# Two extra 2 MB expert slots, and a shorter routing chain, ahead of the mixture of experts

## The chip, the cores and the metric

The kernel runs on one core of one Trainium2 chip, as one launch. The metric is the device time of one execution in microseconds, the lower the better. Engines are called by the names of the profile: PE (TensorE), PEld (its weight loads), DVE (VectorE), ACT (ScalarE), POOL (GpSimd) and SP (SyncE, which here only issues DMAs).

## What is computed

Two transformer blocks over 256 tokens of width 1024, in float32. The change lies at the seam to the last stage, the mixture of experts of the second block, which is this, cut to its core (4 groups of 8 experts, 2 chosen per token, each expert 1024 to 512 to 1024):

```python
p_group = softmax(h @ w_router_group)              # 256 x 4
g_idx, g_gate = argmax(p_group), max(p_group)
logits_sel = (h @ w_router_expert) of group g_idx  # 256 x 8
top_vals, top_idx = top_k(logits_sel, 2)
comb = one_hot(g_idx) * softmax(top_vals) * g_gate
for g in range(G):
    hg = einsum('td,edf->tef', h, w_gate[g])
    hu = einsum('td,edf->tef', h, w_up[g])
    act = silu(hg) * hu * comb[:, g, :, None]
    y = y + einsum('tef,efd->td', act, w_down[g])
```

Here h is the RMS norm of the residual x, and y is added to x.

## The kernel before

Up to 1139 us of the span the kernel runs four dense feed-forward layers and three mixers. Their weights pass through a ring of raw pieces; ACT rounds each piece to fp32r (`high`), DVE takes the rest (`low`), and PE multiplies three times (`product`, L242 to L246). The last of them, `mix_out`, adds its result to x. Then comes the expert stage.

**The experts.** Each of the 32 experts has 6 MB of weights, which are loaded as three pairs of 2 MB: two pairs hold half the rows of gate and up, one pair holds down. A pair is two DMAs of 1 MB, issued by SP in `pair_load` (L1951). The 32 experts are always all loaded, in the order of a plan. The pairs go through `pair_ring`, six slots of 2 MB, laid over `low`, `high`, `raw` and a part of `scratch`. In `moe_sp` SP issues the first pair once the mixer's second tile of h is there (`h_ready`, L1676), the next two once the last piece is split, the next three once PE has used the last piece. Then it waits for the plan (`last_batch`, L1932), and issues each later pair when PE has used the pair six before it (`pair_used`).

**A batch** is four experts ("items") of 32 token slots each. PE gathers a batch's tokens with a product by a one-hot table `picks` (`turn_batch`, L1996, results in `BATCH_X`), ACT copies that to `batch_x` (L2078), and for each item PE computes gate and up (`gate_up`, L2017), ACT and DVE the SiLU and the product, PE the turn (L2024) and `down` (L2036). At the end of a batch `scatter` (L2047) spreads the results, and DVE adds them to x (L2130). All batches are iterations of one `Fori` loop on each engine; here there are eight. Inside a batch, the gather for the next one comes after the second item's gate and up.

**The routing chain** stands between x and the first `picks`. PE turns x (`x_turn_pe`, L389), ACT writes the rounded transpose `hT_high` (L399), DVE `hT_low` (L409), and PE multiplies by the router in 48 matmuls of 36 columns (`route_pe`). DVE then scales the logits (L1776), finds the group and the two experts with their one-hot `takes` (L1818), and signals `picked` (L1822). PE counts and ranks the tokens by expert with five products (L1925, `ranks`; the trace has two records for each); DVE meanwhile writes h, the normed x (`normed_x`, L377, two of 128x1024), and the shares (L1826 to L1831). With the ranks, DVE works out the item and place of every choice (L1834 to L1857), including overflow items for experts with more than 32 tokens, and writes `picks` and `shares` (`picks_of`, L1886 to L1905). After that it makes the plan (L1870 to L1883). The tables lie in `proj`, which is free by then. Most steps wait for the one before, through the helper `step`.

## Time and profile before

| | us |
|---|---|
| median of 3 runs | 1667.09 (1665.92 to 1668.19) |
| profiled execution, device time | 1667.57 |
| its span | 1665.8 |
| PE busy in the span | 1466.4 (88%) |
| DVE busy | 751.3 (45%) |
| ACT busy | 615.1 (37%) |

The page cuts the span into 40 slices of 41.6 us, and gives for each the busy share of every engine, the granted PE clock, the busy share of the 16 DMA engines and the GB/s that they moved. The dense part fills the first 28 slices, the experts the last 12. A busy PE is not PE at its peak, since a matmul's recorded time overlaps its neighbours'. Times in the timelines are counted from the span's start.

### The profile page before, as it was taken

To read this page: it belongs to the slowest core of one execution; us is meant where nothing else is said; L and a number is where in the kernel's file an instruction comes from. 1 tells how busy PE (TensorE), PEld (TensorE's weight loads), DVE (VectorE), ACT (ScalarE), POOL (GpSimd) and SP (SyncE) were. 2 spreads that over 40 slices of the span, in tenths; PEclk is the share of its full clock that TensorE was granted. 3 is DMA by queue.
4 is the path that set the end of the run, shared out by engine and by line. 5 is a ranking of instruction groups with operands and counts; after the bars stand their busy time and mean duration, and the time that the engine had idled before them with its cause. 6 is when DMAs were issued, how large, how long until landed. Compare 5 with 4: busy or idle time off the path is not lost.

```text
span 1665.8 us, 22441 instructions
## 1 busy us (share of the span) xinstructions
PE 1466.4 (88%) x8732; PEld 1124.5 (68%) x8732; DVE 751.3 (45%) x985; ACT 615.1 (37%) x783; POOL 32.6 (2%) x69
## 2 busy tenths in 40 slices
PE   7999999599999999999999999998676767766766
PEld 5888887588888888877788888777544424434433
DVE  4445647845455554565455454685520221221111
ACT  5343545344344543465654344664010011011010
POOL 4000000000000000000010000000000000000000
PEclk9999989999999999999999999999798888979788
DMA  6646544035645555544355555554599999999997
GB/s 214 218 158 214 190 156 171 27 102 186 218 153 200 177 192 186 190 164 151 127 161 199 200 171 182 176 179 189 199 417 417 418 419 417 418 417 418 418 417 298
DMA packets 170764, 396.54 MB, mean 238 GB/s; under 512 B 9507, under 2 KB 107891, under 8 KB 154336
## 3 DMA queue, kind: packets, MB, share of 16 engines
q1 hardware_dynamic: 169152, 392.20, 63.3%
q0 software_dynamic: 1440, 3.72, 0.9%
q8 instruction: 28, 0.46, 0.1%
q14 instruction: 16, 0.13, 0.0%
q10 hardware_dynamic: 128, 0.03, 0.0%
HBM read 393.83 MB, written 1.05 MB: 237 GB/s over the span
## 4 chain that ended last, share of the span: by engine, by line
PE 69%; DMA 11%; SPq 9%; DVE 6%; ACT 3%; issue 2%; DVEq 0%; ACTq 0%
PE psum L244 19%; PE psum L246 19%; PE psum L245 19%; DMA pair_ring<-in_w_exp_up 9%; SPq L1951 9%; PE psum L1996 4%; PE psum L2017 2%; PE psum L2036 1%; DMA pair_ring<-in_w_exp_down 1%; PE psum L526 1%; DVE low L239 1%; DVE hT_low L409 1%; ACT hT_high L399 1%; ACT high L235 1%; PE psum L1162 1%
## 5 line engine op out<-in xcount | busy, mean ns | idle before, releaser
L239 DVE TENSOR_TENSOR low<-raw,high 128x2048 fp32r<-128x2048 f32 x179 | 406.4, 2289 | 138.3 <-ACT high L235 135.3
L244 PE MATMUL psum<-high,hT_high 128*128 128x512 f32 x1088 | 437.2, 402 | 13.8 <-DVE low L2264 5.0
L246 PE MATMUL psum<-high,hT_low 128*128 128x512 f32 x1088 | 428.0, 393 | 0.0
L245 PE MATMUL psum<-low,hT_high 128*128 128x512 f32 x1088 | 427.2, 393 | 0.0
L235 ACT ACTIVATE high<-raw 128x2048 fp32r<-128x2048 f32 x179 | 338.3, 1911 | 61.3 <-PE psum L246 56.7
L244 PEld LDWEIGHTS psum<-high,hT_high 128*128 128x128 f32 x1088 | 206.7, 190 | 59.6 <-issue 8.9
L246 PEld LDWEIGHTS psum<-high,hT_low 128*128 128x128 f32 x1088 | 206.4, 190 | 44.9
L245 PEld LDWEIGHTS psum<-low,hT_high 128*128 128x128 f32 x1088 | 207.1, 190 | 40.8
L2017 PE MATMUL psum<-pair_ring,scratch 128*32 128x256 f32 x2048 | 141.8, 428 | 57.5 <-DMA pair_ring<-in_w_exp_up 56.2
L2017 PEld LDWEIGHTS psum<-pair_ring,scratch 128*32 128x32 f32 x2048 | 67.6, 120 | 129.7 <-DMA pair_ring<-in_w_exp_up 77.8
L636 ACT ACTIVATE aT_high<-psum 128x512 fp32r<-128x512 f32 x40 | 23.9, 598 | 323.0 <-PE psum L526 323.0
L674 DVE TENSOR_TENSOR aT_low<-psum,aT_high 128x512 fp32r<-128x512 f32 x40 | 27.7, 692 | 255.3 <-ACT aT_high L636 255.3
L244 PE MATMUL psum<-high,aT_high 128*128 128x512 f32 x352 | 137.4, 390 | 0.2
L246 PE MATMUL psum<-high,aT_low 128*128 128x512 f32 x352 | 137.0, 389 | 0.0
L245 PE MATMUL psum<-low,aT_high 128*128 128x512 f32 x352 | 137.0, 389 | 0.0
L2036 PE MATMUL psum<-pair_ring,scratch 128*32 128x256 f32 x1024 | 82.8, 478 | 44.9 <-DMA pair_ring<-in_w_exp_down 40.7
L2087 ACT ACTIVATE scratch<-psum 32x256 f32<-32x256 f32 x64 | 23.8, 373 | 200.3 <-PE psum L2036 199.9
L2109 DVE TENSOR_TENSOR scratch<-scratch,psum 128x128 f32<-128x128 f32 x32 | 9.2, 287 | 186.8 <-ACT scratch L2082 186.8
L2036 PEld LDWEIGHTS psum<-pair_ring,scratch 128*32 128x32 f32 x1024 | 40.8, 131 | 72.8 <-issue 52.6
L2082 ACT ACTIVATE scratch<-psum 128x128 f32<-128x128 f32 x32 | 8.9, 277 | 212.1 <-PE psum L2017 212.1
L1996 PE MATMUL psum<-proj,h 128*128 128x128 f32 x288 | 71.1, 408 | 8.2 <-DVE proj L1904 8.2
L1996 PEld LDWEIGHTS psum<-proj,h 128*128 128x128 f32 x288 | 69.4, 335 | 12.9 <-issue 12.9
(317 smaller groups left out, 1173.7 us busy)
## 6 DMA issues: line engine op xcount, KB each, us to landing
pair_ring<-in_w_exp_gate SPq DMA_DIRECT2D x64, 1024.0 KB, 22.1
pair_ring<-in_w_exp_up SPq DMA_DIRECT2D x64, 1024.0 KB, 22.8
pair_ring<-in_w_exp_down SPq DMA_DIRECT2D x64, 1024.0 KB, 22.4
raw<-in_ffn_w_gate SPq DMA_DIRECT2D x88, 512.0 KB, 4.1
raw<-in_ffn_w_up SPq DMA_DIRECT2D x88, 512.0 KB, 5.3
raw<-in_ffn_w_down SPq DMA_DIRECT2D x88, 512.0 KB, 4.0
raw<-in_gla_w_in SPq DMA_DIRECT2D x24, 512.0 KB, 4.6
raw<-in_sb_w_in SPq DMA_DIRECT2D x24, 512.0 KB, 4.6
```

Source lines behind the costliest of these rows:

```text
L235: act.activation(high[:, p % RING, :], raw_of(p), ACT.Copy).then_inc(rounded, 1)
L239: dve.tensor_tensor(low[:, p % RING, :], raw_of(p), high[:, p % RING, :].bitcast(F32), ALU.subtract).then_inc(split, 1)
L244: pe.matmul(psum_out, lhs_high, rhs_high, start=start, stop=False, skip_group_check=True)
L245: pe.matmul(psum_out, lhs_high, rhs_low, start=False, stop=False, skip_group_check=True)
L246: return pe.matmul(psum_out, lhs_low, rhs_high, start=False, stop=stop, skip_group_check=True)
L636: act.activation(flat(aT_high), TURN_A, ACT.Copy).then_inc(a_high, 1)
L674: dve.tensor_tensor(flat(aT_low), TURN_A, flat(aT_high).bitcast(F32), ALU.subtract).then_inc(a_low, 1)
L1951: sp.dma_start(dst, src).then_inc(pair_landed[i % PAIRS], 16)
L1996: ins = pe.matmul(BATCH_X[:, k * P:(k + 1) * P], h[:, tt, :].rearrange("p (n k) -> p k n", k=KD)[:, k, :], picks[:, tt * P:(tt + 1) * P], ...
L2017: ins = pe.matmul(out_rows, batch_x[:, kk, j * SLOTS:(j + 1) * SLOTS], w[:, :, k, c * P:(c + 1) * P], start=kk == 0, stop=kk == KD - 1, sk ...
L2036: ins = pe.matmul(ITEM_Y[q * SLOTS:(q + 1) * SLOTS, :], item_aT[:, c * SLOTS:(c + 1) * SLOTS], w[:, c, q * QUARTER:(q + 1) * QUARTER], sta ...
L2087: ins = act.activation(batch_y[j * SLOTS:(j + 1) * SLOTS, q * QUARTER:(q + 1) * QUARTER], ITEM_Y[q * SLOTS:(q + 1) * SLOTS, :], ACT.Copy)
```

## The change

- **Memory.** `gate`, `act_tok` and `proj` now stand right behind `aT_high` and `aT_low`, and `extra_pairs`, two slots of 2 MB, is laid over these five. `hT_high` and `hT_low` become one buffer, and the routing tables move from `proj` to `route_tables`, laid over it; `iota` and `group_pad` move to `levels`.
- **Loads.** SP issues pairs 6 and 7 first, into the extra slots, at the point where pair 0 was issued; then pair 0, and pairs 1 to 5 behind the waits that they had. Pairs 8 to 11 wait for the first four uses and not for the plan; their experts, 2 and 3, are fixed. From the second batch on, the ring of six serves alone, and each pair waits for the use of the pair six before.
- **Router product.** For each k one matmul of 72 columns (high and low router side by side) and one of 36, instead of three of 36: 32 matmuls for 48. DVE adds the two halves before it scales.
- **Order.** ACT takes the second tile's mean square after its transpose. DVE writes h ahead of the wait for the logits, not behind `picked`.
- **First batch.** Its slots are 32 times the expert plus the rank; a rank of 32 or more is pushed out of range by `too_far`. `picks_of(0)` thus comes right after the ranks, and the item arithmetic runs behind it.
- **PE program.** The first batch is written out, and the loop runs over the others; PE reads the plan after the first batch.


The diff, cut to its core:

```diff
+EXTRA = 2
...
-        hT_high = sb("hT_high", [P, KD, TOKENS], F32R)
-        hT_low = sb("hT_low", [P, KD, TOKENS], F32R)
+        hT = sb("hT", [P, 2, KD * TOKENS], F32R)
+        hT_high, hT_low = (hT[:, i, :].rearrange("p (k n) -> p k n", k=KD) for i in range(2))
+        route_tables = nc.alloc_sbuf_tensor_at("route_tables", [P, 2 * KD * TOKENS], F32, offset=tables_at)
+        extra_at = -(-nc.sbuf_base // 32) * 32
         aT_high = sb("aT_high", [P, 2, TOKENS], F32R)
         aT_low = sb("aT_low", [P, 2, TOKENS], F32R)
+        gate = sb("gate", [P, TT, CHUNK])
+        act_tok = sb("act_tok", [P, TT, CHUNK])
+        proj = sb("proj", [P, TT, GLA_COLS])
+        extra_pairs = nc.alloc_sbuf_tensor_at("extra_pairs", [P, EXTRA, PAIR], F32, offset=extra_at)
...
+        router_parts = sb("router_parts", [P, KD, 2, GROUPS + EXPERTS], F32R)
+        router_high, router_low = router_parts[:, :, 0, :], router_parts[:, :, 1, :]
...
                 load_roots(act)
+                mean_act(act, 8, 0)
                 for tt in range(TT):
-                    mean_act(act, 8, tt)
                     x_turn_act(act, 8, tt)
+                mean_act(act, 8, 1)
                 root_act(act, 8)
...
         def route_dve(dve, step):
             dve.wait_ge(e["tables"], 1)
             dve.memset(group_pad, -3e38)
+            for tt in range(TT):
+                normed_x(dve, 8, tt)
+            dve.wait_ge(e["logits"], 1)
             dve.memset(plan_f, 0.0)
-            dve.wait_ge(e["logits"], 1)
...
+            step(dve.tensor_copy(by_tile(logits_low), parts[:, :, 1, :]))
             have_rstd(dve, 8)
             for tt in range(TT):
-                ins = dve.tensor_scalar(logits[:, tt * n:(tt + 1) * n], ROUTE[:, tt * n:(tt + 1) * n], rstd[:, tt:tt + 1], None,
-                                        ALU.mult)
+                c = slice(tt * n, (tt + 1) * n)
+                ins = dve.tensor_tensor(logits[:, c], parts[:, tt, 0, :], logits_low[:, c], ALU.add)
+            step(ins)
+            for tt in range(TT):
+                c = slice(tt * n, (tt + 1) * n)
+                ins = dve.tensor_scalar(logits[:, c], logits[:, c], rstd[:, tt:tt + 1], None, ALU.mult)
             step(ins)
...
-            for tt in range(TT):
-                normed_x(dve, 8, tt)
+            dve.tensor_scalar(first_slot, pick, float(SLOTS), None, ALU.mult)
...
             dve.wait_ge(e["ranks"], 1)
             step(dve.tensor_copy(counts, ROUTE[:, CNT:CNT + 3 * EXPERTS]))
+            def at_choice(table, to):
...
+            at_choice(rank, place_of)
+            dve.tensor_tensor(first_slot, first_slot, place_of, ALU.add)
+            step(dve.tensor_scalar(too_far, place_of, SLOTS - 0.5, float(P * SLOTS), ALU.is_gt, ALU.mult))
+            step(dve.tensor_tensor(from_slot, first_slot, too_far, ALU.add))
+            picks_of(dve, 0)
...
-            step(dve.scalar_tensor_tensor(slot_of, item_of, float(SLOTS), place_of, ALU.mult, ALU.add))
-            step(dve.tensor_scalar(from_slot, slot_of, float(P), None, ALU.add))
-            picks_of(dve, 0)
+            at_choice(item, item_of)
+            at_choice(place_in, place_of)
+            step(dve.scalar_tensor_tensor(from_slot, item_of, float(SLOTS), place_of, ALU.mult, ALU.add))
...
-                    ins = product(pe, ROUTE[:, tt * n:(tt + 1) * n], hT_high[:, k, tok], hT_low[:, k, tok],
-                                  router_high[:, k, :], router_low[:, k, :], start=tt == 0 and k == 0)
+                    pe.matmul(ROUTE[:, tt * 2 * n:(tt + 1) * 2 * n], hT_high[:, k, tok],
+                              router_parts[:, k, :, :].rearrange("p i n -> p (i n)"), start=tt == 0 and k == 0, stop=False,
+                              skip_group_check=True)
+                    ins = pe.matmul(ROUTE[:, tt * 2 * n:tt * 2 * n + n], hT_low[:, k, tok], router_high[:, k, :],
+                                    start=False, stop=False, skip_group_check=True)
...
+        def slot(i, b):
+            if b == 0:
+                return i if i < PAIRS else (i - PAIRS - EXTRA) % PAIRS
+            return (i - EXTRA) % PAIRS
...
         def moe_sp(sp):
+            sp.wait_ge(h_ready, H_AT["n8"])
+            for i in range(PAIRS, PAIRS + EXTRA):
+                pair_load(sp, i, 0, i // 3)
             for i in range(PAIRS):
-                if i == 0:
-                    sp.wait_ge(h_ready, H_AT["n8"])
-                elif i == 1:
+                if i == 1:
                     sp.wait_ge(split, MOE)
                 elif i == 3:
                     sp.wait_ge(used, MOE)
-                pair_load(sp, i, i // 3)
+                pair_load(sp, i, 0, i // 3)
+            for i in range(PAIRS + EXTRA, PER_BATCH):
+                sp.wait_ge(pair_used, i - PAIRS - EXTRA + 1)
+                pair_load(sp, i, 0, i // 3)
             n = last_batch(sp)
...
+                    b = (c, 1)
+                    sp.wait_ge(pair_used, at(b, PER_BATCH, 3 * i + j - PAIRS + 1))
+                    pair_load(sp, 3 * i + j, b, expert)
...
             pe.wait_ge(h_ready, H_AT["n8"] + TT)
             turn_batch(0)
-            turn_shares(0)
-            n = last_batch(pe)
-            with pe.Fori(0, n + 1) as b:
+            turn_shares()
+            batch(0, 1)
+            n = last_batch(pe)
+            with pe.Fori(0, n) as c:
+                batch((c, 1), (c, 2))
```

Three places show what moved. First, DVE from the `picked` step (L1822) to the copy of counts and ranks (L1834); L377 writes h:

```order
L1822 TENSOR_TENSOR proj<-proj 128x64
L377 SCALAR_TENSOR_TENSOR h<-x,rstd,gain 128x1024 x2
L1826 TENSOR_REDUCE proj<-proj 128x2
L1827 RECIPROCAL proj<-proj 128x2
L1828 TENSOR_SCALAR proj<-proj 128x2
L1829 RECIPROCAL proj<-proj 128x2
L1830 TENSOR_TENSOR proj<-proj 128x2
L1831 TENSOR_TENSOR proj<-proj 128x2
L1834 COPY proj<-psum 128x96
```

Now, under the new line numbers (`picked` is L1838, the copy L1849; L1839 begins the slots of the first batch):

```order
L1838 TENSOR_TENSOR route_tables<-route_tables 128x64
L1839 TENSOR_SCALAR route_tables<-route_tables 128x4
L1841 TENSOR_REDUCE route_tables<-route_tables 128x2
L1842 RECIPROCAL route_tables<-route_tables 128x2
L1843 TENSOR_SCALAR route_tables<-route_tables 128x2
L1844 RECIPROCAL route_tables<-route_tables 128x2
L1845 TENSOR_TENSOR route_tables<-route_tables 128x2
L1846 TENSOR_TENSOR route_tables<-route_tables 128x2
L1849 COPY route_tables<-psum 128x96
```

The two of L377 are gone from here to a place ahead of the wait for the logits.

Second, DVE ahead of the first tables (L1895 writes the first of them; L1854 and L1856 look up the item and the place of each choice; nine operations between the copy and these rows are left out):

```order
L1850 TENSOR_TENSOR proj<-proj 128x64
L1851 SCALAR_TENSOR_TENSOR proj<-proj 128x64
L1852 TENSOR_TENSOR proj<-proj 128x64
L1854 TENSOR_TENSOR proj<-proj 128x128
L1856 TENSOR_REDUCE proj<-proj 128x4
L1854 TENSOR_TENSOR proj<-proj 128x128
L1856 TENSOR_REDUCE proj<-proj 128x4
L1857 SCALAR_TENSOR_TENSOR proj<-proj 128x4
L1859 TENSOR_SCALAR proj<-proj 128x4
L1888 TENSOR_SCALAR proj<-proj 128x4
L1895 TENSOR_SCALAR proj<-proj 128x128
L1896 TENSOR_SCALAR proj<-proj 128x128
```

Now, from the copy (L1849) to the tables (L1916):

```order
L1849 COPY route_tables<-psum 128x96
L1852 TENSOR_TENSOR route_tables<-route_tables 128x128
L1854 TENSOR_REDUCE route_tables<-route_tables 128x4
L1857 TENSOR_TENSOR route_tables<-route_tables 128x4
L1858 TENSOR_SCALAR route_tables<-route_tables 128x4
L1859 TENSOR_TENSOR route_tables<-route_tables 128x4
L1916 TENSOR_SCALAR route_tables<-levels,route_tables 128x128
L1917 TENSOR_SCALAR route_tables<-levels,route_tables 128x128
```

Five operations stand between the copy and the tables, where 19 did; the others run behind the tables.

Third, SP's queue at the start of the experts (the `x8` are the last dense weights):

```order
L229 DMA raw<-in_w_out 128x1024 x8
L1951 DMA pair_ring<-in_w_exp_gate 128x2048
L1951 DMA pair_ring<-in_w_exp_up 128x2048
L1951 DMA pair_ring<-in_w_exp_gate 128x2048
L1951 DMA pair_ring<-in_w_exp_up 128x2048
L1951 DMA pair_ring<-in_w_exp_down 128x2x1024 x2
```

SP now (L1993 is `pair_load`):

```order
L235 DMA raw<-in_w_out 128x1024 x8
L1993 DMA extra_pairs<-in_w_exp_gate 128x2048
L1993 DMA extra_pairs<-in_w_exp_up 128x2048
L1993 DMA extra_pairs<-in_w_exp_gate 128x2048
L1993 DMA extra_pairs<-in_w_exp_up 128x2048
L1993 DMA pair_ring<-in_w_exp_gate 128x2048
L1993 DMA pair_ring<-in_w_exp_up 128x2048
L1993 DMA pair_ring<-in_w_exp_gate 128x2048
L1993 DMA pair_ring<-in_w_exp_up 128x2048
L1993 DMA pair_ring<-in_w_exp_down 128x2x1024 x2
```

Two pairs into `extra_pairs`, four DMAs, stand ahead of pair 0. Not shown: the plan's read, L1956, has come to stand behind pairs 8 to 11.

## Rows read from the trace of the kernel before

**Rows 1.** The page, DMA issues: count, KB each, median us from issue to landing.
```profile
pair_ring<-in_w_exp_up SPq DMA_DIRECT2D x64, 1024.0 KB, 22.8
```

**Rows 2.** Stretches: engines' busy us, PEclk, DMA share, GB/s in the last columns.
```profile
1139.80:1150.10 10.30, 10.30 (x51) 8.63 (x50) 5.87 (x4) 3.38 (x5) 0.00 (x0) 1.00 0.56 204
1150.10:1179.00 28.90, 20.63 (x113) 18.67 (x111) 15.45 (x67) 8.41 (x24) 0.24 (x1) 0.76 0.91 363
1179.00:1196.80 17.80, 10.21 (x74) 9.27 (x78) 10.20 (x40) 2.31 (x2) 0.00 (x0) 0.72 0.00 0
1196.80:1205.00 8.20, 7.10 (x129) 3.83 (x117) 3.63 (x13) 1.02 (x3) 0.00 (x0) 1.00 0.84 291
1205.00:1650.00 445.00, 314.89 (x3242) 180.74 (x3238) 77.72 (x204) 46.21 (x104) 0.00 (x0) 0.87 1.02 418
1650.00:1654.00 4.00, 1.18 (x13) 0.60 (x13) 0.58 (x2) 1.20 (x2) 0.00 (x0) 0.88 0.36 144
```

**Rows 3.** Timeline of SP's queue: start, duration, line, load issued.
```profile
1139.80 0.33 SPq L1951 DMA_DIRECT2D pair_ring<-in_w_exp_gate  x1
...
1150.13 0.33 SPq L1951 DMA_DIRECT2D pair_ring<-in_w_exp_gate  x1
...
1159.86 0.34 SPq L1951 DMA_DIRECT2D pair_ring<-in_w_exp_gate  x1
...
1196.82 0.37 SPq L1951 DMA_DIRECT2D pair_ring<-in_w_exp_gate  x1
...
1217.36 0.35 SPq L1951 DMA_DIRECT2D pair_ring<-in_w_exp_gate  x1
```

**Rows 4.** Timeline of DVE, routing: start, duration, line, operation, and idle before.
```profile
1163.50 2.16 DVE L409 SCALAR_TENSOR_TENSOR hT_low<-psum,gainT,hT_high 128x128 fp32r<-128x128 f32 x8 [2.24 <-ACT hT_high L399]
...
1170.30 0.17 DVE L1781 COPY proj<-proj 128x8 f32<-128x8 f32 x1
...
1174.76 0.23 DVE L1822 TENSOR_TENSOR proj<-proj 128x64 f32<-128x64 f32 x1
1174.90 2.47 DVE L377 SCALAR_TENSOR_TENSOR h<-x,rstd,gain 128x1024 f32<-128x1024 f32 x2
...
1178.33 0.26 DVE L1834 COPY proj<-psum 128x96 f32<-128x96 f32 x1
...
1181.39 0.29 DVE L1854 TENSOR_TENSOR proj<-proj 128x128 f32<-128x128 f32 x1
...
1183.29 0.28 DVE L1895 TENSOR_SCALAR proj<-proj 128x128 f32<-128x128 f32 x1
```

**Rows 5.** Timeline of PE from the routing to the first expert product.
```profile
1169.21 0.38 PE L245 MATMUL psum<-router_low,hT_high 128*128 128x36 f32 x1
1169.43 0.38 PE L246 MATMUL psum<-router_high,hT_low 128*128 128x36 f32 x1
1175.04 1.06 PE L1925 MATMUL psum<-proj,ones 128*128 128x32 f32 x4 [5.24 <-DVE proj L1822]
...
1176.77 0.61 PE L1925 MATMUL psum<-proj,strict 128*128 128x32 f32 x2
1185.61 7.88 PE L1996 MATMUL psum<-proj,h 128*128 128x128 f32 x32 [8.23 <-DVE proj L1904]
...
1194.68 0.64 PE L2017 MATMUL psum<-pair_ring,scratch 128*32 128x256 f32 x8 [0.97 <-ACT scratch L2078]
```

**Rows 6.** Timeline of ACT at the second token tile.
```profile
1161.29 1.06 ACT L341 ACTIVATE square<-x 128x1024 f32<-128x1024 f32 x1 [2.39 <-DVE x L325]
...
1164.34 0.34 ACT L355 ACTIVATE rms<-mean_sq,eps 128x2 f32<-128x2 f32 x1
```

**Rows 7.** DMA queues that fetch instructions, 1195 to 1260 us: packets, MB.
```profile
q8 instruction: 3, 0.05, 0.3%
q14 instruction: 2, 0.02, 0.1%
```

**Rows 8.** The same, 1260 to 1640 us.
```profile
q14 instruction: 1, 0.01, 0.0%
```

128 lines of the change are left out of this document (68 added, 60 removed).

## The prediction, made before the change was run

> **What bounds the kernel now.** I read the stretches first, then SP's queue, then the chain of single operations on DVE, PE and ACT that ends before the first expert product.
>
> The stretches [rows 2] show a stage that is bound by its loads. From 1205 to 1650 us the DMA engines are busy all the time (share 1.02) at 418 GB/s, while PE is busy 315 of 445 us. 32 experts of three pairs are 96 pairs of 2.097 MB, so a pair is worth 2.097 / 0.418 = 5.02 us, and all of them 482 us. Each load takes 22.8 us from issue to landing [rows 1], which is more than four pairs of 5.02 us: the ring always has work queued. What PE does in these 445 us costs nothing. The stage can only be shortened by bytes that move earlier, or by an earlier start of this unbroken stream.
>
> Before it the stream is broken. The first issue is at 1139.80, the next at 1150.13, the next at 1159.86, and then none until 1196.82 [rows 3]. 204 GB/s over 10.3 us is 2.1 MB, pair 0; 363 GB/s over 28.9 us is 10.5 MB, pairs 1 to 5; and from 1179 to 1196.8 nothing moves at all [rows 2]. All six slots are full, and the first is freed when PE has done half of the first expert, which starts at 1194.68 [rows 5]. From 1196.8 to 1205 the engines moved 291 x 8.2 = 2.39 MB, worth 5.7 us at full rate, so the unbroken stream counts as begun at 1205 - 5.7 = 1199.3. At its end 144 x 4 = 0.58 MB come after 1650, so it ends at 1651.4: 452.1 us for 90 pairs, 5.02 each. Behind it lies a tail of 1665.8 - 1651.4 = 14.4 us (last down product, scatter, store), which the change leaves alone.
>
> So the end is: begin of the stream + pairs left at that point x 5.02 + 14.4. The change works on both of the first two.
>
> **Part 1: two pairs more in the idle time.** SP issues pairs 6 and 7, then 0, at 1139.80. Pairs 1 and 2, and then 3, 4 and 5, are issued when they were. Before, all six were in by 1179 [rows 2]; two more make that 1179 + 10.0 = 1189 at the latest. If the engines never pause from 1141 on, it is 1141 + 8 x 5.02 = 1181, and since the first three pairs, 15.1 us, now bridge the pause between the first two issues, I take that end. Either is before the first freed slot at about 1191 (below), so the two fit into time in which nothing moves now, and 88 pairs are left instead of 90. Worth 2 x 5.02 = **10.0 us**. PE needs pair 0 first, at about 1189, and it is there by about 1160. The cost of the four DMA issues on SP, 0.33 us each [rows 3], falls where SP waits for the next event.
>
> The Trainium skill, "DMA: Bandwidth & Descriptors", section "Where 436 GB/s comes from", says that for loads from HBM the HBM side binds, at about 358 GB/s per core. By that a pair would be 5.86 us, part 1 an estimated 11.7 us, and the sum below 1650.1. The trace does not agree: 418 GB/s held for 445 us [rows 2]. I go by the trace.
>
> **Part 2: the chain to the first tables.** PE's first gather starts at 1185.61, right behind the tables that begin at 1183.29 [rows 4, 5]. Three pieces move.
>
> *Logits.* ACT now does the second tile's mean square behind the transpose. It held the transpose by about 1.1 us (1161.29, 1.06 long) [rows 6], so hT_high and hT_low come 1.1 us earlier, hT_low at 1162.4 instead of 1163.50 [rows 4]. PE's matmuls of 36 columns are 0.22 us apart there at the low clock (1.2 GHz level, 0.50 granted) [rows 5]; 16 instead of 24 behind the last transpose are 3.5 us instead of 5.2. They would end near 1167.2. But DVE now writes h first: the root is done at about 1165.0 (1164.34 + 0.34 before, the same operations in another order) [rows 6], with the reciprocal 1165.2, and the two of L377 take 2.47 us [rows 4]: 1167.7. Then five more small operations to the scaled logits, some 0.23 each: 1168.9, against 1170.30 [rows 4]. Gain 1.4 us. If a matmul of 72 columns costs twice one of 36, PE ends at 1163.6 + 8 x 0.66 = 1168.9, and the gain shrinks to 0.3; if the clock stays high, DVE still ends last, so 1.6 is the top.
>
> *Ranks.* From `picked` to the copy of the ranks DVE took 1178.33 - 1174.76 = 3.57 us, because L377 stood in between [rows 4]. Without it the shares are only about 1.1 us, and the ranks come last: PE started 0.28 us after L1822 began and needed from 1175.04 to 1177.38 (1176.77 + 0.61) [rows 5], so 2.7 us in all. Gain 0.9 us; a wait takes the place of most of the L377 that goes.
>
> *Slots from ranks.* From the copy to the first table, 1178.33 to 1183.29, are 20 operations in 4.96 us, 0.25 each [rows 4]. Now it is the copy and five: 6 x 0.25 = 1.5 us. Gain 3.5 us; at worst, with 0.3 for each of the wide ones, 3.2.
>
> Sum 1.4 + 0.9 + 3.5 = **5.8 us**, between 4.3 and 6.2. What follows is unchanged: the gather of 7.88 us, ACT's copy, and the first product 9.07 us after the gather's start [rows 5]. I take the gather as equally long although it may run at another clock. So the first product starts at 1188.9, the first reload is issued at 1191.0, and the stream counts as begun at 1193.5.
>
> **What is moved behind.** The item arithmetic and the plan now stand behind the tables, 17 and 14 operations. The tables are done at 1179.8; 31 operations of 0.25 to 0.35 us make the plan ready between 1187.5 and 1190.6. ACT and DVE wait for it ahead of their loops. Their first work there is the SiLU of the first item, which needs both halves of its gate and up. One half took 2.1 us (1194.68 to the reload at 1196.82) [rows 3, 5], so the SiLU is due at 1188.9 + 4.2 = 1193.1, at least 2.5 us later than the plan. SP does not need the plan before pair 12, nor PE before the second batch. I cost the move at nothing; without this cover, each us that the plan is late would hold DVE and ACT, and PE behind them.
>
> **Does the stream stay unbroken?** Pair 12 goes by the ring of six, so it waits for the seventh use, although its slot is free after the fifth. The seventh use came 1217.36 - 1196.82 = 20.5 us after the first [rows 3]. Pairs 8 to 11 keep the engines busy for 20.1 us, from 2.5 us after the first reload's issue (1199.3 - 1196.82). So the engines go dry at +22.6, and pair 12, issued at +20.5, needs to flow within 2 us. It just does. I cost it at 0, with 2 us as its upper end.
>
> **The sum.** 10.0 + 5.8 = 15.8. Against the profiled execution's own 1667.57 this gives 1651.8; the median of the runs shown lies 0.5 lower, at 1667.09. I forecast **1651.4**.
>
> **Rivals.**
>
> *A. The chain gives less* (0.09). The 72-column matmuls or the ranks on PE end last, or the waits between DVE's small operations grow. Part 2 gives 2 to 4 us instead of 5.8: 1653.5 to 1655.5. For it speaks that PE is at the low clock through the whole chain; against it that each operation has its row.
>
> *B. The stream breaks at pair 12* (0.05). If PE's first batch is slower by a few us than before (its instructions are new, its third item reads another buffer), every us of it counts at once. With 2 to 4 us: 1653.5 to 1655.5.
>
> *C. The chain is not what starts the stream* (0.01), and only the pairs count, or the first slots are filled late. Then only 10.0 is gained: 1657.
>
> *D. Slower* (0.03). PE's first batch is written out, so its some 400 matmuls with their weight loads are fetched once more than a loop body is. If a block of instructions queues behind loads that are in the rings, it lands like a load, 22.8 us [rows 1]. One such stall of PE while SP has two pairs out leaves the engines dry for 22.8 - 10.0 = 12.8 us and the gain is nearly gone, 1664.2; two make 25.6, and the time 1677. It decides from 15.8 us of dry rings on. Against it: three and two instruction blocks were fetched from 1195 to 1260 with the rings full, and PE showed no wait for anything but data [rows 7]; and the rings are empty until 1193.5, when most of the batch's code is read.
>
> The Trainium skill, "Runtime: NRT & Kernel Launch", section "Instruction fetch mechanics", says that a taken branch out of the loaded pages forces a fetch, and that straight code is fetched ahead. The change takes the branch in the second batch, with full rings. In the trace, 380 us with six turns of the loop show a single fetch [rows 8], so a turn does not cost one. By the rule alone a late stall would fall into PE's slack and give the time of the sum.
>
> *E. More than forecast* (0.02): 1648 to 1649, if the stream's begin also loses its hesitation of 2.5 us.
>
> **How the numbers follow.** The forecast case has 0.80, with bounds 4.3 to 6.2 on part 2 and 0 to 2 on the break: 1651.0 to 1654.9. The range takes in A, B and half of E: 1649.0 to 1656.0. A measurement of this kernel can tell about 0.2%, 3.3 us, from no change. All cases but D, and a small rest, lie beyond that: faster 0.95, same 0.02, slower 0.03.
>
> **What would show it.** Right: only one idle stretch of the DMA engines, 10 to 12 us up to a reload at about 1191; h written ahead of the logits; the copy of the ranks waiting for PE; the first table 1.5 us behind that copy instead of 5.0; then 418 GB/s without a dip until about 1635.5, tail 14.4 us. Wrong: a dip in GB/s around 1213 (B); a wait of DVE for PE at the logits (A); PE idle in the first batch with its data landed (D); a rate below 418.

## The result, and the profile after

The changed kernel took **1652.67 us** (median of 4 runs, 1651.71 to 1654.07), the kernel before 1667.64 in the same session (4 runs, 1665.92 to 1668.68): a ratio of 0.9911, 95% interval 0.9899 to 0.9922. The forecast was 1651.4, its range 1649.0 to 1656.0. The profiled execution took 1652.77 us with a span of 1651.0.

The page of the changed kernel: the granted clock and the rate in 40 slices, the queue of instructions, and the loads.

```profile
PEclk9999989899999999999999999999799888989888
...
GB/s 214 215 166 202 205 153 155 49 89 191 197 184 197 181 157 215 166 178 153 128 153 209 177 204 179 153 180 199 292 412 417 416 418 419 417 417 418 419 417 295
...
q8 instruction: 32, 0.52, 0.1%
...
pair_ring<-in_w_exp_up SPq DMA_DIRECT2D x62, 1024.0 KB, 22.8
```

The first thing to see is that nothing about the bound has changed: the nine slices ahead of the last stand at 416 to 419 GB/s, and a load still takes 22.8 us, as in [rows 1]. The same stretches as in [rows 2], with the limits where this trace has its events (the granted clock, the DMA share and GB/s are the last three columns):

```profile
1180.00:1182.00 2.00, 2.00 (x10) 2.00 (x10) 1.75 (x9) 0.00 (x0) 0.00 (x0) 0.50 0.62 248
1182.00:1184.00 2.00, 2.00 (x10) 2.00 (x10) 1.83 (x6) 0.00 (x0) 0.00 (x0) 0.50 0.03 10
1184.00:1192.00 8.00, 7.11 (x56) 4.99 (x58) 3.55 (x13) 2.31 (x2) 0.00 (x0) 0.74 0.00 0
1192.00:1194.00 2.00, 1.50 (x28) 0.65 (x20) 0.12 (x1) 0.28 (x1) 0.00 (x0) 1.00 0.57 100
1212.00:1214.00 2.00, 2.00 (x40) 0.97 (x32) 0.00 (x0) 0.00 (x0) 0.00 (x0) 1.00 1.09 358
1214.00:1216.00 2.00, 0.90 (x17) 0.48 (x17) 0.58 (x2) 0.28 (x1) 0.00 (x0) 1.00 0.89 346
1230.00:1630.00 400.00, 277.51 (x2935) 156.99 (x2937) 72.32 (x192) 40.85 (x93) 0.00 (x0) 0.89 1.02 418
1635.00:1640.00 5.00, 3.90 (x37) 1.53 (x33) 0.58 (x2) 1.20 (x2) 0.00 (x0) 0.50 0.29 117
```

The engines now move expert bytes until about 1181; the stretch in which they move nothing is 10 us long (1182 to 1192) where it was 17.8. From 1194 on the stream is at full rate, with one dip: 358 and 346 GB/s from 1212 to 1216. It ends at 1636.3 (the bytes after 1630, at 418). SP's queue, as [rows 3]:

```profile
1139.34 0.33 SPq L1993 DMA_DIRECT2D extra_pairs<-in_w_exp_gate  x1
...
1149.66 0.33 SPq L1993 DMA_DIRECT2D pair_ring<-in_w_exp_gate  x1
...
1159.37 0.34 SPq L1993 DMA_DIRECT2D pair_ring<-in_w_exp_gate  x1
...
1161.18 31.53 SPq L1993 DMA_DIRECT2D pair_ring<-in_w_exp_down  x4
1193.56 0.34 SPq L1993 DMA_DIRECT2D pair_ring<-in_w_exp_gate  x1
...
1212.53 0.37 SPq L1993 DMA_DIRECT2D pair_ring<-in_w_exp_gate  x1
```

The two extra pairs go out first, then pair 0. The row at 1161.18 joins four down loads: the last two of them, pair 8 in an extra slot, are the first reload and went out at 1191.82. Pair 12 follows at 1212.53. DVE, as [rows 4]:

```profile
1162.16 2.16 DVE L415 SCALAR_TENSOR_TENSOR hT<-psum,gainT,hT 128x128 fp32r<-128x128 f32 x8 [1.39 <-ACT hT L405]
...
1164.81 2.48 DVE L383 SCALAR_TENSOR_TENSOR h<-x,rstd,gain 128x1024 f32<-128x1024 f32 x2
...
1167.27 0.18 DVE L1785 COPY route_tables<-psum 128x72 f32<-128x72 f32 x1
...
1168.24 0.17 DVE L1797 COPY levels<-route_tables 128x8 f32<-128x8 f32 x1
...
1172.70 0.23 DVE L1838 TENSOR_TENSOR route_tables<-route_tables 128x64 f32<-128x64 f32 x1
...
1175.43 0.26 DVE L1849 COPY route_tables<-psum 128x96 f32<-128x96 f32 x1 [1.50 <-PE psum L1949]
...
1176.84 0.28 DVE L1916 TENSOR_SCALAR route_tables<-levels,route_tables 128x128 f32<-128x128 f32 x1
...
1178.67 0.35 DVE L1925 SCALAR_TENSOR_TENSOR route_tables<-route_tables 128x128 f32<-128x128 f32 x1
...
1187.24 0.19 DVE L1904 CAST route_tables<-route_tables 128x49 int32<-128x49 f32 x1
```

PE, as [rows 5]:

```profile
1172.98 1.06 PE L1949 MATMUL psum<-route_tables,ones 128*128 128x32 f32 x4 [6.71 <-DVE route_tables L1838]
...
1174.71 0.61 PE L1949 MATMUL psum<-route_tables,strict 128*128 128x32 f32 x2
1179.16 7.88 PE L2045 MATMUL psum<-route_tables,h 128*128 128x128 f32 x32 [3.84 <-DVE route_tables L1925]
...
1188.16 5.35 PE L2066 MATMUL psum<-pair_ring,scratch 128*32 128x256 f32 x64 [0.89 <-ACT scratch L2131]
```

and ACT, as [rows 6], where the second tile's mean square (L347) now stands behind the eight transposes (L405):

```profile
1160.99 2.17 ACT L405 ACTIVATE hT<-psum,gainT 128x128 fp32r<-128x128 f32 x8 [2.57 <-PE psum L395]
1163.00 1.11 ACT L347 ACTIVATE square<-x 128x1024 f32<-128x1024 f32 x1
```

Between executions the first expert load is issued anywhere from 1139.3 to 1141.5 us, in work ahead of the change. So every event below is counted from that issue. This ledger is read from the timelines of all the traces; the experiments in it are told below. "Gate+up" is the first expert product. "Stream" is the end of the loads: 1630 us plus what the one-microsecond stretches behind it moved, at 418 GB/s. "Tail" is from there to the end of the span.

| trace | gather | gate+up starts, takes | stream | tail | span from the first issue |
|---|---|---|---|---|---|
| before | 45.81 | 54.88, 3.66 | 511.4 | 14.6 | 526.0 |
| change | 39.82 | 48.82, 5.35 | 497.0 | 14.7 | 511.7 |
| change_again | 40.11 | 49.11, 3.66 | 495.6 | 14.4 | 510.1 |
| no_extra | 40.11 | 49.10, 3.66 | 505.2 | 14.4 | 519.6 |
| one_extra | 39.85 | 48.84, 5.35 | 501.6 | 14.4 | 515.9 |
| old_chain | 45.48 | 54.48, 3.66 | 501.2 | 17.6 | 518.9 |
| late_picks | 43.00 | 52.00, 3.66 | 498.6 | 16.8 | 515.4 |
| mean_square_first | 40.65 | 49.65, 5.34 | 498.4 | 14.9 | 513.4 |
| h_late | 39.73 | 48.73, 3.66 | 495.4 | 17.4 | 512.8 |
| three_products | 40.13 | 49.13, 3.66 | 496.0 | 13.2 | 509.2 |
| own_slot_wait | 39.85 | 48.85, 5.35 | 496.4 | 12.6 | 509.0 |
| warm_pe | 39.00 | 48.00, 3.66 | 494.7 | 14.6 | 509.3 |
| waits_and_warm | 38.99 | 47.98, 3.66 | 493.9 | 15.4 | 509.3 |
| warm_to_the_end | 38.80 | 47.80, 3.66 | 495.0 | 19.9 | 514.9 |

One reading of it carries the case. Take from "stream" the end of the first gate+up. The eight traces with 88 pairs left that keep the change's waits give 442.8 to 443.4 us (change, change_again, old_chain, late_picks, mean_square_first, h_late, three_products, warm_pe), whether the product took 3.66 or 5.35. One pair fewer loaded early gives 447.4, two fewer 452.5. So the stage is one length, set by the pairs left, hung on the end of the first product. The change and change_again are one kernel; their gathers lie 0.3 us apart, so a difference of that size between two traces tells nothing.

### The profile page after: what moved, and what is told of

It reads as the page before. It is cut to its first block, busy times and chain, and to the rows that moved or that the text cites. A ratio compares the mean times of both kernels' runs of the same rounds, so it can differ in the third digit from the quotient of the medians.

```text
span 1651.0 us, 22368 instructions
## 1 busy us (share of the span) xinstructions
PE 1456.6 (88%) x8716; PEld 1115.4 (68%) x8716; DVE 752.7 (46%) x992; ACT 615.3 (37%) x783; POOL 30.8 (2%) x69
## 3 DMA queue, kind: packets, MB, share of 16 engines
q0 software_dynamic: 1440, 3.72, 1.0%
## 4 chain that ended last, share of the span: by engine, by line
PE 70%; DMA 11%; SPq 8%; DVE 6%; ACT 3%; issue 2%; DVEq 0%; ACTq 0%
PE psum L250 19%; PE psum L252 19%; PE psum L251 19%; DMA pair_ring<-in_w_exp_up 9%; SPq L1993 8%; PE psum L2045 4%; PE psum L2066 2%; PE psum L2085 2%; DMA pair_ring<-in_w_exp_down 1%; PE psum L532 1%; DVE low L245 1%; ACT hT L405 1%; ACT high L241 1%; DVE hT L415 1%; PE psum L1169 1%
## 5 line engine op out<-in xcount | busy, mean ns | idle before, releaser
L250 PE MATMUL psum<-high,hT 128*128 128x512 f32 x1088 | 436.2, 401 | 14.1 <-DVE low L2317 5.0
L252 PE MATMUL psum<-high,hT 128*128 128x512 f32 x1088 | 427.5, 393 | 0.0
L251 PE MATMUL psum<-low,hT 128*128 128x512 f32 x1088 | 427.0, 392 | 0.0
L250 PEld LDWEIGHTS psum<-high,hT 128*128 128x128 f32 x1088 | 206.4, 190 | 59.8 <-issue 8.9
L252 PEld LDWEIGHTS psum<-high,hT 128*128 128x128 f32 x1088 | 206.0, 189 | 44.5
L251 PEld LDWEIGHTS psum<-low,hT 128*128 128x128 f32 x1088 | 206.5, 190 | 40.5
L2066 PE MATMUL psum<-pair_ring,scratch 128*32 128x256 f32 x1984 | 140.4, 434 | 56.7 <-DMA pair_ring<-in_w_exp_up 55.6
L2066 PEld LDWEIGHTS psum<-pair_ring,scratch 128*32 128x32 f32 x1984 | 66.2, 122 | 128.4 <-DMA pair_ring<-in_w_exp_up 76.7
L2085 PE MATMUL psum<-pair_ring,scratch 128*32 128x256 f32 x1024 | 79.6, 464 | 42.7 <-DMA pair_ring<-in_w_exp_down 37.7
L2085 PEld LDWEIGHTS psum<-pair_ring,scratch 128*32 128x32 f32 x1024 | 36.6, 128 | 73.1 <-DMA pair_ring<-in_w_exp_down 30.1
L250 PEld LDWEIGHTS psum<-high,aT_high 128*128 128x128 f32 x352 | 66.1, 188 | 14.5 <-DVE aT_low L684 0.9
L252 PEld LDWEIGHTS psum<-high,aT_low 128*128 128x128 f32 x352 | 66.1, 188 | 13.8
## 6 DMA issues: line engine op xcount, KB each, us to landing
pair_ring<-in_w_exp_up SPq DMA_DIRECT2D x62, 1024.0 KB, 22.8
```

The costliest lines, as they stand in the source:

```text
L250: pe.matmul(psum_out, lhs_high, rhs_high, start=start, stop=False, skip_group_check=True)
L251: pe.matmul(psum_out, lhs_high, rhs_low, start=False, stop=False, skip_group_check=True)
L252: return pe.matmul(psum_out, lhs_low, rhs_high, start=False, stop=stop, skip_group_check=True)
L2066: ins = pe.matmul(out_rows, batch_x[:, kk, j * SLOTS:(j + 1) * SLOTS], w[:, :, k, c * P:(c + 1) * P], start=kk == 0, stop=kk == KD - 1, sk ...
L2085: ins = pe.matmul(ITEM_Y[q * SLOTS:(q + 1) * SLOTS, :], item_aT[:, c * SLOTS:(c + 1) * SLOTS], w[:, c, q * QUARTER:(q + 1) * QUARTER], sta ...
```

## The experiments

The medians stand beside runs of the kernel before on the same chip: four kernels with 1669.33 (7 runs), four with 1667.88 (7 runs), four with 1668.69 (9 runs).

**How much are the pairs?** One number was changed, in no_extra to 0 and in one_extra to 1. (In no_extra the buffer `extra_pairs` also had to keep one slot, which nothing uses.)

```diff
-EXTRA = 2
+EXTRA = 0
```

> The changed kernel with no extra slot (EXTRA = 0), all else kept: the shorter chain alone. If each extra pair is worth one pair of the unbroken stream (5.02 us), the end comes 10.0 us later than in the changed kernel: about 1662.7. If the extra pairs bought less, because part of their time was already covered or because the six-slot ring's late wait at the second batch costs something only with extras, it is less: 1660 to 1661.5. The dip in GB/s around 1213 us should be gone.

> One extra slot instead of two. Additive theory: half of the way, 5.0 us later than the changed kernel, about 1657.7. Rival (the second pair is worth less than the first, since its room before the first freed slot is short): nearer to the changed kernel, 1653 to 1655.

no_extra took 1661.37 us (1660.61 to 1662.79), ratio 0.9956 [0.9939, 0.9973]; one_extra 1657.09 (1655.82 to 1657.47), ratio 0.9929 [0.9913, 0.9946]. From end of product to end of stream the first extra pair shortens by 5.1 us (452.5 to 447.4) and the second by 4.6 (447.4 to 442.8). Neither trace shows a dip around the issue of the pair that first goes round the ring; the change does, and its dip is what the second pair is short by. The gather stands where the change's two traces have it (39.85 in one_extra, 40.11 in no_extra), so the two parts of the change don't touch each other.

**How much is the chain, and which part of it?** old_chain keeps the two extra pairs and writes the routing as before: mean square ahead of the transposes, three products of 36 columns, h behind `picked`, slots behind the item arithmetic. late_picks undoes only the last of these: the block that makes the slots from the ranks goes, and the table is written where it was.

```diff
-            at_choice(rank, place_of)
-            dve.tensor_tensor(first_slot, first_slot, place_of, ALU.add)
...
-            picks_of(dve, 0)
...
             step(dve.scalar_tensor_tensor(from_slot, item_of, float(SLOTS), place_of, ALU.mult, ALU.add))
+            picks_of(dve, 0)
```

> Both extra slots, but the routing chain as before: three router matmuls per k, mean square ahead of the second transpose, h written behind the choice of experts, first tables behind the item arithmetic. If the chain's gain goes to the stream one for one: 5.8 to 6.0 us later than the changed kernel, about 1658.5. If the start of the stream is set by something else: no difference. Extras and chain together should add up to the whole difference of 15 us.

> The changed kernel, but the first tables are written behind the item arithmetic again (slots of the first batch from items and places). My count says 3.5 us on the chain for this one part, so 3.5 us later: about 1656.2, and the first reload 3.5 us later. Rival: the three parts of the chain overlap, and one part alone undone costs less, 2 us or under.

old_chain took 1657.80 us (1655.62 to 1660.40), 0.9932 [0.9915, 0.9948]; late_picks 1656.35 (1655.04 to 1657.44), 0.9925 [0.9909, 0.9942]. Their gathers, first the one of old_chain, then that of late_picks:

```profile
1185.22 7.88 PE L2032 MATMUL psum<-route_tables,h 128*128 128x128 f32 x32 [7.91 <-DVE route_tables L1915]
```

```profile
1183.07 7.88 PE L2041 MATMUL psum<-route_tables,h 128*128 128x128 f32 x32 [6.98 <-DVE route_tables L1921]
```

Their first issues were at 1139.74 and 1140.07, so the gathers come 45.48 and 43.00 us behind them, where the change's two traces have 39.82 and 40.11. The whole chain is worth 5.4 to 5.7 us at the gather (against before 6.0), and the slots alone 2.9 to 3.2: less than the 3.5 that was expected, but well above the rival's 2. By the ratios the two lie 3.5 and 2.3 us above the change, with intervals some 5 us wide, so the medians alone would say little of the parts.

**h ahead of the logits, the two-part logits, the mean square.** h_late moves the two instructions of L383 back behind `picked`; three_products writes the router as three products of 36 columns, and drops DVE's copy and two additions that joined the halves; mean_square_first puts the second mean square ahead of the transposes again.

```diff
+++ h_late
-            for tt in range(TT):
-                normed_x(dve, 8, tt)
...
             dve.tensor_tensor(takes_any, takes[:, 0:half], takes[:, half:], ALU.add).then_inc(e["picked"], 1)
+            for tt in range(TT):
+                normed_x(dve, 8, tt)
+++ mean_square_first
-                mean_act(act, 8, 0)
                 for tt in range(TT):
+                    mean_act(act, 8, tt)
                     x_turn_act(act, 8, tt)
-                mean_act(act, 8, 1)
```

> The changed kernel, but DVE writes h behind the choice of experts again. The logits then start when PE ends them, 1.0 us earlier, and the 2.5 us of h fall into the time in which PE makes the ranks. Theory: no difference at the first gather (within 0.2 us), since h only fills a wait in either place. Rival (my count of the part): 0.9 us or more later.

> The changed kernel with the router product as before: three matmuls of 36 columns per k into one sum, and DVE scales it straight from PSUM, without the copy and the two additions. PE then ends the logits at about 1167.5 instead of 1166.2, but DVE is held by its writing of h until 1167.3 in either case and saves 0.55 us of small operations. Theory: this part of the change is worth nothing, 0.3 us earlier to 0.1 us later at the first gather. Rival (as I had counted the part): the extra matmuls cost 0.3 us or more.

> Only the order on ACT undone: the mean square of the second tile again ahead of its transposes. Theory 1 (the prediction): the transposes are read 1.1 us later, but DVE with h and the reciprocal also waits for the root, which stays where it is, so the logits are ready 0.3 to 1.1 us later and the gather comes 0.3 to 1.1 us later after the first issue than the 39.8 us of the change. Theory 2 (DVE with h ends last at the logits, and hides it): 0 to 0.2 us. Either way 1652.8 to 1654.0 us, the trace tells them apart and the median hardly does.

h_late took 1653.82 us (1653.35 to 1656.06), 0.9914 [0.9897, 0.9930]; three_products 1651.06 (1650.92 to 1651.23), 0.9898 [0.9881, 0.9914]; mean_square_first 1653.15 (1651.12 to 1656.74), 0.9906 [0.9891, 0.9921]. None differs from the change by its median; the traces do better. PE in h_late:

```profile
1174.18 1.06 PE L1949 MATMUL psum<-route_tables,ones 128*128 128x32 f32 x4 [5.81 <-DVE route_tables L1836]
...
1181.27 7.88 PE L2045 MATMUL psum<-route_tables,h 128*128 128x128 f32 x32 [4.75 <-DVE route_tables L1925]
```

With h behind `picked` the ranks start 32.64 us after the first issue, where the change has 33.64 and change_again 33.93: 1.0 to 1.3 earlier. The gather starts at 39.73 against 39.82 and 40.11: of the gain 0.1 to 0.4 is left. Moving h ahead lengthens the logits by 1.0 to 1.3, because DVE and not PE then ends last there (the copy at 1167.27 stands right behind L383, with no idle time ahead of it), and gives 0.9 back at the ranks, which no longer wait behind L383. The move is worth nothing by itself, and may cost up to 0.4.

three_products has its gather at 40.13 and mean_square_first at 40.65: 0 to 0.3 and 0.5 to 0.8 behind the change's two traces. So the mean square's place is worth something, as its theory 1 had it, and three_products falls between its two theories (0.1 or less; 0.3 or more) and decides nothing. The single edits sum to 3.1 to 4.2, the whole to 5.4 to 5.7. A reason is at hand: with h in front, DVE covers part of PE's logits, so an edit there shows fully only when h is late too. No run has that pair, and it stays an argument.

**The two shortfalls.** In the trace of the change the stream ended 497.0 us after the first issue, 1.4 later than the kernel before less the forecast's sum (511.4 - 15.8 = 495.6). Two causes were in the trace: the first gate+up took 5.35 us instead of 3.66, and the stream dips where pair 12 is issued. Each has an experiment: warm_pe for the product, own_slot_wait for the dip. own_slot_wait lets pairs 12 and 13 wait for the use of their own slot (fifth and sixth) instead of the seventh and eighth, with the loads of the second batch written out. warm_pe has TensorE do idle products in a free bank, 7 behind the logits and 4 behind the ranks.

```diff
+++ own_slot_wait
+            for i in range(TILES):
...
+                for j in range(3):
+                    k = 3 * i + j
+                    sp.wait_ge(pair_used, PER_BATCH + k - PAIRS + 1 - (EXTRA if k < EXTRA else 0))
+                    pair_load(sp, k, 1, expert)
...
-            with sp.Fori(0, n) as c:
+            with sp.Fori(0, n - 1) as c:
+++ warm_pe
+        def keep_warm(pe, times):
+            for _ in range(times):
+                pe.matmul(banks(5)[:, 0:TOKENS], ones[:, 0:P], ones[:, :], start=True, stop=True, skip_group_check=True)
...
+            keep_warm(pe, 7)
...
+            keep_warm(pe, 4)
```

> The changed kernel, but pairs 12 and 13 wait only for the uses that free their own slots, the fifth and the sixth, instead of the seventh and eighth; the second batch's loads are written out for that. Theory: the dip to 350 GB/s between 1212 and 1216 us comes from that wait; it goes, and with it 0.6 to 1.0 us of the time. Rival: the dip belongs to PE's pace or to the DMA engines, and stays; no difference.

> The changed kernel with 7 idle products (128x256, into an unused PSUM bank) behind the logits and 4 behind the ranks, in time in which PE otherwise waits for DVE. Theory: PE's granted clock was 0.5 from 1164 to 1185 us and again from 1188 to 1191, because PE had waited; kept at work it stays at 1.0, the five rank products take 1.2 us instead of 2.3, and the first gate and up 3.66 us instead of 5.35: 1.5 to 2.5 us earlier at the first reload, about 1650.5 in the end. Rival: the clock falls all the same, and the added products only stand in the way of the ranks: 0 to 1 us slower.

own_slot_wait took 1650.83 us (1650.52 to 1652.08), 0.9899 [0.9883, 0.9916]; warm_pe 1651.16 (1649.03 to 1651.77), 0.9895 [0.9878, 0.9912]. In own_slot_wait pair 12 goes out at 1201.97, ten microseconds earlier:

```profile
1201.97 0.36 SPq L1993 DMA_DIRECT2D pair_ring<-in_w_exp_gate  x1
```

and the stretches of the dip read

```profile
1212.00:1214.00 2.00, 2.00 (x44) 1.23 (x40) 0.00 (x0) 0.00 (x0) 0.00 (x0) 1.00 1.04 418
1214.00:1216.00 2.00, 0.90 (x17) 0.22 (x13) 0.58 (x2) 0.28 (x1) 0.00 (x0) 1.00 1.03 420
```

The dip is gone, and the stream ends 442.2 us after the first product instead of 442.8 to 443.4. What the change lost there, (60 + 72) GB/s over 2 us each, is 0.26 MB, 0.63 us at 418 GB/s. Both ways the wait is worth 0.6 in a stream that begins like this one. In warm_pe PE reads:

```profile
1167.18 6.11 PE L1931 MATMUL psum<-ones 128*128 128x256 f32 x14
1174.38 0.63 PE L1954 MATMUL psum<-route_tables,ones 128*128 128x32 f32 x4 [1.08 <-DVE route_tables L1838]
...
1175.30 0.39 PE L1954 MATMUL psum<-route_tables,strict 128*128 128x32 f32 x2
...
1179.52 7.89 PE L2051 MATMUL psum<-route_tables,h 128*128 128x128 f32 x32 [1.06 <-DVE route_tables L1925]
...
1188.52 3.66 PE L2072 MATMUL psum<-pair_ring,scratch 128*32 128x256 f32 x64 [0.90 <-ACT scratch L2137]
```

The ranks' last product ends 1.3 us after their start instead of 2.3, the gather comes 39.00 us after the first issue instead of 39.82, its own length stays at 7.89, and the first gate+up takes 3.66. But the clock did not stay up, as the theory had it. It fell to 0.50 while PE did the idle products, and again at the gather:

```profile
1168.00:1172.00 4.00, 4.00 (x10) 3.12 (x10) 3.64 (x22) 0.21 (x1) 0.00 (x0) 0.50 1.02 426
1180.00:1182.00 2.00, 2.00 (x10) 2.00 (x10) 1.76 (x9) 0.00 (x0) 0.00 (x0) 0.50 1.02 410
```

From 1174 to 1176, when the ranks ran, it was 1.00, and from 1184 on again. The short ranks are well borne out: in all three traces with idle products their first row takes 0.63 us, in all the others 1.06. The short first product is not: it came in three traces of three, but also in six of the ten traces of changed kernels without idle products, so three in a row can be chance.

**Both together, and the tail.** The last four ran on one chip, with the change itself among them (change_again). waits_and_warm has both edits; warm_to_the_end adds idle products in the fourth item of each batch.

```diff
+                    if j == 3 and half:
+                        if b != 0:
+                            pe.wait_ge(e["added"], at(b, TT, 0))
+                        keep_warm(pe, 16)
...
+                if j == 3:
+                    keep_warm(pe, 8)
                 pair_there(pe, i, b)
```

> The change itself, unaltered, beside the three below on one chip. Both theories expect 0.9911 of the kernel before (0.990 to 0.992), about 1652.8 us, the first gate and up product at 5.35 us or at 3.66 us by the granted clock, and a dip of 0.6 to 1.0 us in the stream where pair 12 is issued.

> Pairs 12 and 13 wait for the use that frees their own slot, and TensorE does idle products behind the logits and behind the ranks. Theory 1 (the two shortfalls are separate and both lie on the path): no dip around pair 12 (0.6 to 1.0 us), the first gate and up at the 2.4 GHz level (1.7 us), ranks 0.5 us shorter: 2 to 3 us below the change, 1650.3 us, about 0.9894. Theory 2 (the dip only appears when the stream starts late against PE, so that one mend takes the other's gain): 1.0 to 1.7 us below the change, no better than either alone, 1651.2 us.

> As the one above, and in the fourth item of each batch 16 idle products between the two halves of gate and up and 8 ahead of the down product, in time in which TensorE waits for loads. Theory 1 (the granted clock at the end is set by how busy TensorE is, and it prices the tail): the last down product takes 1.93 us instead of 3.64, the scatter 3.67 instead of up to 5.95, the tail is 12.7 to 14 us, the stream is as before at 418 GB/s; 0.5 to 2 us below the run above. Theory 2 (the clock at the end falls for another reason, or the slack is not there): no change within 0.5 us, the granted clock still 0.50 in parts of 1630 to 1650, or a stream that breaks because pairs are freed later: 1 to 3 us above.

change_again took 1652.43 us (1649.38 to 1655.18), 0.9900 [0.9885, 0.9916]; waits_and_warm 1651.02 (1649.94 to 1653.02), 0.9897 [0.9882, 0.9912]; warm_to_the_end 1655.47 (1655.01 to 1657.02), 0.9923 [0.9909, 0.9936].

change_again ran its first product at the 2.4 GHz level. The stretch of its dip, then that product:

```profile
1214.00:1216.00 2.00, 1.07 (x17) 0.31 (x9) 0.46 (x2) 0.28 (x1) 0.00 (x0) 1.00 0.93 293
```

```profile
1190.53 3.66 PE L2066 MATMUL psum<-pair_ring,scratch 128*32 128x256 f32 x64 [0.89 <-ACT scratch L2131]
```

Its stream ends 495.6 us after the first issue, 1.3 before the first trace of the same kernel, and its dip is the same (293 GB/s for 2 us, 0.6 us). In waits_and_warm the stream ends at 493.9: 1.7 before change_again and 3.0 before the change. Of the 1.7, 1.1 is there at the gather (38.99 against 40.11) and 0.6 comes from the product's end to the stream's (442.3 against 442.9). So the two mends add up to the end of the stream, and neither takes the other's gain. As a size, 1.7 is the upper end of theory 2, and 3.0 fits theory 1 only against the trace with the slow first product. The medians (1651.02 against 1652.43) can't decide either: the tail of that trace was 15.4 us, where own_slot_wait had 12.6. The products behind the stream, waits_and_warm first, own_slot_wait second:

```profile
1637.50 3.54 PE L2103 MATMUL psum<-pair_ring,scratch 128*32 128x256 f32 x32 [2.10 <-DMA pair_ring<-in_w_exp_down]
1642.08 3.67 PE L2114 MATMUL psum<-scratch 128*128 128x512 f32 x8 [1.03 <-ACT scratch L2158]
```

```profile
1637.81 1.93 PE L2097 MATMUL psum<-pair_ring,scratch 128*32 128x256 f32 x32 [0.58 <-DMA pair_ring<-in_w_exp_down]
1640.77 3.67 PE L2108 MATMUL psum<-scratch 128*128 128x512 f32 x8 [1.02 <-ACT scratch L2152]
```

The same last down product is 3.54 us or 1.93, the scatter 3.67 in both and 5.88 in h_late. The tail runs from 12.6 to 17.6 us over the traces without idle products in it, longest where the last products find the low level, and a gain of 0.6 to 1.7 us ahead of it can't be told by four or five runs.

warm_to_the_end was to settle that and missed by its own price. (In the loop it also waits for the last batch's additions to x; no idle time stands ahead of the first row below.) PE at the end:

```profile
1630.13 7.17 PE L1931 MATMUL psum<-ones 128*128 128x256 f32 x32
1637.24 1.93 PE L2088 MATMUL psum<-pair_ring,scratch 128*32 128x256 f32 x32
...
1640.61 3.72 PE L1931 MATMUL psum<-ones 128*128 128x256 f32 x16 [0.38 <-DVE scratch L2188]
1644.26 1.93 PE L2109 MATMUL psum<-pair_ring,scratch 128*32 128x256 f32 x32
1647.23 3.67 PE L2120 MATMUL psum<-scratch 128*128 128x512 f32 x8 [1.04 <-ACT scratch L2164]
```

The clock was as theory 1 said: 1.00 in every stretch from 1630 to 1640, down product 1.93, scatter 3.67. But 16 idle products of 256 columns in fp32 took 7.17 us, 0.45 each, and the 8 took 3.72. The waits in which they were to hide are 1.5 to 3.1 us in the other traces. So 4 us and more of idle work came behind the last loads, and the tail grew to 19.9. In the loop they cost a little too: the stream ends 443.5 us after the first product, 1.2 later than in waits_and_warm. I had sized the idle product by the expert products, which take 0.11 us each (32 in 3.66). A smaller dose at the end was not tried.

## Why the prediction was right

The range held the time, and the time lies 1.3 us above the number. The kernel before was itself 0.55 us slower in that session (1667.64) than the 1667.09 that the forecast started from; the difference of the medians is 15.0 us, 0.8 short of the sum of 15.8. Step by step:

*Two pairs, 10.0 us.* Right, and the rate with it: 418 GB/s from 1230 to 1630. no_extra against change_again, whose first products are alike, is 9.6 us at the end of the stream, and 10.2 once the 0.6 of the dip is added. The extra bytes were all in by about 1181, the end that the forecast took; 1180 to 1182 still show 248 GB/s, 1182 to 1184 only 10. The Trainium skill, "DMA: Bandwidth & Descriptors", section "Where 436 GB/s comes from", says that the HBM side binds such loads at about 358 GB/s. By that a pair would be an estimated 5.86 us; the pairs measured 4.6 to 5.1, and the trace held 418 GB/s.

*The chain, 5.8 us.* The gather came 5.99 us earlier after the first issue. By its pieces: the copy of the logits to `levels` 28.90 us after that issue (30.50 before): 1.60, forecast 1.4. From `picked` to the copy of the ranks 2.73 us (3.57 before): 0.84, forecast 0.9, and the copy does wait for PE, 1.50 us. From there to the first table 1.41 (4.96 before): 3.55, forecast 3.5. The fear that 72 columns cost twice 36 did not come true. What the forecast did not see is that the first two pieces are tied: the 0.84 at the ranks was paid for with 1.0 to 1.3 at the logits, so that the chain would have been as short with h left where it was (h_late).

*The plan behind the tables, at nothing.* The tables end at 1179.0, the plan at 1187.4, just ahead of the forecast's 1187.5 to 1190.6. ACT and DVE need it for work that comes after the first product, and that began at 1188.16. Right.

*"What follows is unchanged: the gather of 7.88 us, ACT's copy, and the first product."* This is **the step that failed**, by 1.7 us in the shown trace. The gather was 7.88 again at either clock, and the first product began 9.00 us after it. But the product itself took 5.35 us instead of 3.66: the granted clock was 0.56 and 0.59 from 1188 to 1192 (one trace row below), where in the kernel before it was 1.00 from 1190 on, ahead of its product at 1194.68. In the change it had been 1.00 as well, from 1186 to 1188, and fell again.

```profile
1188.00:1190.00 2.00, 1.84 (x20) 0.98 (x24) 0.00 (x0) 1.39 (x2) 0.00 (x0) 0.56 0.00 0
1190.00:1192.00 2.00, 2.00 (x28) 0.99 (x24) 0.00 (x0) 0.00 (x0) 0.00 (x0) 0.59 0.00 0
```

The forecast said that the gather might run at another clock and took it as equal. It should have asked so of the product, whose time does change with the clock. It does not come with the change each time: of the traces that have the whole change, one shows 5.35 and one 3.66, and of the eight other changed kernels without idle products three show 5.34 or 5.35. Where PE did idle products ahead of it, in three traces of three, it was 3.66. What decides between the two stays open: the kernel is the same in the change and change_again.

*"It just does. I cost it at 0, with 2 us as its upper end."* Missed by 0.6 us, inside its bound. The comparison used a start of the flow 2.5 us behind the first reload, taken from before. Here the flow counted as begun at 1193.5, 1.7 behind the reload at 1191.82. The engines then go dry at 1.7 + 20.1 = 21.8 us, and pair 12, issued 20.7 behind, flows at 20.7 + 1.7 = 22.4. That is the gap of 0.6 that the stretches show. In the eight traces that keep this wait and both extra pairs the stream ends 423.8 to 424.4 us after the issue of pair 12. So a small dip stands for a bound: from pair 12 on, its wait sets the stream. Two more traces bear that out. In warm_pe and three_products the flow counts as begun 2.4 and 2.5 us behind the first reload, as the forecast took it, and there is no such dip (395 and 418 GB/s, 418 and 403, from 1212 to 1216); yet the stream ends the same 424.0 and 424.2 us behind pair 12.

*The sum.* With the first product as in the kernel before, the span from the first issue fell by 526.0 - 510.1 = 15.9 us (change_again), forecast 15.8; in the trace of the change it fell by 14.3. In the latter, the product at the low level (1.7) and the dip (0.6) work against 0.2 more from the chain and 0.8 from the shorter hesitation of the stream's begin, which is the part of rival E that came true. That change_again lies within 0.1 of the forecast is in part luck: the dip and the shorter hesitation were both costed at nothing, and they nearly cancel, since an earlier begin runs into the wait of pair 12.

*The rivals.* A did not happen: none of its waits did, and the single operations kept their price. B did at a quarter of its price, and in another way than told: PE's batch was not slower, the margin was. C, that the chain does not start the stream, fell with old_chain, which lies behind change_again by 5.4 us at the gather and by 5.6 at the end of the stream. D fell: the instruction queues took 32 packets and 0.52 MB where the kernel before had 28 and 0.46, and PE's idle stretches in its first batch all end on ACT or DVE, none longer than 1.1 us. The Trainium skill, "Runtime: NRT & Kernel Launch", section "Instruction fetch mechanics", speaks of a fetch where a branch leaves the loaded pages; no run here shows a time for it.

## What to carry to other kernels

When a stage is one unbroken stream of loads, write its end as (event that lets it begin) + (bytes left) / (rate) and look for edits of either term: here they added to the microsecond. When a ring of slots is lengthened by slots outside it, look at the first slot that goes round: a wait written for the ring alone was late by half a microsecond, and it set the rest of the stream. And when an operation moves ahead of another to clear a wait, follow the engine that now ends last: the gain at the second wait may be paid at the first.

## What the runs showed of the hardware

- The clock that is granted to TensorE after a pause differs from run to run of one kernel. It moved the first product between 3.66 and 5.35 us, the last down product between 1.93 and 3.64, the scatter between 3.67 and 5.95, and so the tail between 12.6 and 17.6 us. That is about as much as this kernel's times scatter (1649.4 to 1655.2 in change_again). Idle products did not keep the clock up (0.50 from 1168 to 1172 in warm_pe, with PE busy all the time); the ranks behind them ran at 1.00 in three traces of three.
- The gather, 32 products of 128 columns with strided weights, takes 7.88 or 7.89 us however the clock stands: in the kernel before, ten of its records fall in 1186 to 1188, at 0.50, and ten in 1190 to 1192, at 1.00.
- A router product of 72 columns is followed by the next as soon as one of 36: in the trace of the change they start 0.11 us apart at the high level and 0.21 at the low one, and those of 36 columns in the kernel before 0.21 apart at the low one too. So the number of products, not of columns, is what counts there. (At the gather it was worth 0 to 0.3 us, since DVE ends last.)
- An idle product of 128x128 weights and 256 columns in fp32 takes 0.45 us at the high level, four times one of the expert products with 128x32 weights and the same columns (0.11). What makes the difference was not tried apart: the expert products also write to four different groups of output rows in turn.
